# Each expert's rows spread by products on four row groups of the array, and five transfers and copies moved

## The reference

```python
def first_block(x, c, ...):
    mod = silu(c) @ w_ada + b_ada            # six rows: shift, scale, gate, twice
    h = rmsnorm(x, g_pre_mix) * (1 + scale_m) + shift_m
    # w_in projection; retention and dilated attention; mixed = [y_ret, y_att] @ w_out
    x = x + gate_m * rmsnorm(mixed, g_post_mix)
    h = rmsnorm(x, g_pre_ffn) * (1 + scale_f) + shift_f
    affinity = softmax(h @ w_router)                       # 16 experts
    gates, idx = top_k(affinity.T, 32)                     # each expert takes 32 tokens
    ye = (silu(h[idx] @ w_gate) * (h[idx] @ w_up)) @ w_down * gates
    moe = zeros_like(h).at[idx].add(ye)
    return x + gate_f * rmsnorm(moe, g_post_ffn)
# then, twice: half an FFN (1024 -> 2816 -> 1024), an mLSTM and windowed attention
# with a relative position bias, half an FFN, and a per-layer embedding.
```

## Time and profile before

| | before |
|---|---|
| three runs | 2316.99 to 2321.66 us, median 2320.9 |
| the profiled execution | 2319.57 us, its span 2317.8 us |
| PE, DVE, ACT busy | 81%, 46%, 30% of the span |
| mean granted clock of PE | 0.90 |
| HBM read | 656.6 MB, 284 GB/s over the span |

### The profile page before, as it was taken

One profiled execution on the slowest core, in us unless ns is written; L12 is line 12 of the kernel. 1 busy time (PEld: TensorE's weight loads), 2 busy tenths in 40 slices (PEclk: granted clock), 3 DMA queues, 4 the chain that ended last, 5 costly groups with the idle time before them and its releaser, 6 DMA issues.

```text
span 2317.8 us, 30979 instructions
## 1 busy us (share of the span) xinstructions
PE 1886.3 (81%) x11483; PEld 1285.3 (55%) x11483; DVE 1073.8 (46%) x1500; ACT 698.0 (30%) x965; POOL 43.3 (2%) x68
## 2 busy tenths in 40 slices
PE   6896765566555556556699999999999999999999
PEld 4774311111121112111388888788878888778887
DVE  3464100000000000000388877688868887777886
ACT  4331100000000000000344456454454445544444
POOL 0000000000000000000000010000000001000000
PEclk8996977777788877777899999999999999999999
DMA  9786999999999999999755654545545575444552
GB/s 368 259 321 275 429 429 428 429 428 429 428 428 428 428 429 428 429 428 429 310 191 181 234 178 128 175 153 179 201 146 191 172 241 179 136 142 165 184 189 83
DMA packets 174820, 660.83 MB, mean 285 GB/s; under 512 B 10051, under 2 KB 108140, under 8 KB 143732
## 3 DMA queue, kind: packets, MB, share of 16 engines
q1 hardware_dynamic: 171980, 654.12, 72.9%
q10 hardware_dynamic: 2376, 3.03, 0.6%
q0 software_dynamic: 352, 2.11, 0.3%
HBM read 656.60 MB, written 2.64 MB: 284 GB/s over the span
## 4 chain that ended last, share of the span: by engine, by line
PE 55%; DMA 38%; DVE 4%; ACT 2%; issue 1%; ACTq 0%; DVEq 0%; PEldq 0%; SPq 0%; PEld 0%
PE PS L1992 26%; DMA turned_and_rows<-in_w_down_e 13%; PE PS L2080 12%; DMA turned_and_rows<-in_w_gate_e 12%; DMA turned_and_rows<-in_w_up_e 11%; PE PS L2082 6%; PE PS L1948 3%; DVE arena L210 2%; PE PS L1671 2%; DVE units L210 1%; PE PS L1968 1%; DMA ring<-in_w_in 1%; DMA ring<-in_w_ada 1%; ACT units L210 1%; PE PS L2128 1%
## 5 line engine op out<-in xcount | busy, mean ns | idle before, releaser
L210 ACT ACTIVATE units<-ring 128x1024 fp32r<-128x1024 f32 (+2 forms) x416 | 438.4, 1054 | 489.9 <-PE PS L2082 266.4
L210 DVE TENSOR_TENSOR units<-ring,units 128x1024 fp32r<-128x1024 f32 (+2 forms) x416 | 505.9, 1216 | 117.1 <-ACT units L210 82.4
L2080 PE MATMUL PS<-hT_split,units 128*128 128x512 f32 x1216 | 432.4, 398 | 0.0
L210 DVE SCALAR_TENSOR_TENSOR arena<-arena,PS 128x512 f32<-128x512 f32 (+1 forms) x54 | 41.4, 768 | 770.6 <-ACT arena L210 489.6
L210 ACT ACTIVATE arena<-PS 128x512 f32<-128x512 f32 (+3 forms) x137 | 67.7, 494 | 919.9 <-PE PS L1956 309.4
L2082 PE MATMUL PS<-hT_split,units 128*128 128x256 f32 x1216 | 341.3, 281 | 0.0
L1992 PE MATMUL PS<-units,hT_split 128*128 128x512 f32 (+2 forms) x1248 | 285.1, 386 | 4.5 <-DVE hT_split L210 2.5
L2080 PEld LDWEIGHTS PS<-hT_split,units 128*128 128x128 f32 x1216 | 228.5, 188 | 55.9
L1992 PEld LDWEIGHTS PS<-units,hT_split 128*128 128x128 f32 x1248 | 230.5, 189 | 49.2 <-issue 4.4
L1992 PE MATMUL PS<-units,hid_split 128*128 128x512 f32 x1056 | 255.4, 391 | 0.0
L2082 PEld LDWEIGHTS PS<-hT_split,units 128*128 128x128 f32 x1216 | 229.6, 189 | 3.0
(11 more groups left out here) (214 smaller groups left out, 1430.8 us busy)
## 6 DMA issues: line engine op xcount, KB each, us to landing
ring<-in_ffn_wi SPq DMA_DIRECT2D x88, 1024.0 KB, 5.5
ring<-in_w_gate_e SPq DMA_DIRECT2D x24, 2048.0 KB, 36.7
moe_ring<-in_w_up_e SPq DMA_DIRECT2D x24, 2048.0 KB, 36.2
ring<-in_w_down_e SPq DMA_DIRECT2D x24, 2048.0 KB, 35.5
moe_ring<-in_w_gate_e SPq DMA_DIRECT2D x24, 2048.0 KB, 35.9
ring<-in_w_up_e SPq DMA_DIRECT2D x24, 2048.0 KB, 35.8
moe_ring<-in_w_down_e SPq DMA_DIRECT2D x24, 2048.0 KB, 36.2
ring<-in_ffn_wo SPq DMA_DIRECT2D x44, 1024.0 KB, 5.0
```

The source lines that it names most:

```text
L210: return instruction(*args, **kwargs)
L2080: first = mm(PS[:, bank, :].rearrange("p (i n) -> p i n", i=2), w[0], hT_split[:, :, k, :], start=(k == 0), stop=False, skip_group_check=True)
```

## The change

- **Combine.** Each expert's rows are added by themselves. ACT makes one 128x256 copy `Y_e` of bank 5, in which each quarter of the columns stays on its 32 partitions. DVE writes the expert's gated one-hot columns four times side by side (`gated_e`), PE transposes them into bank 5 beside the result, DVE copies them to `GT_e`. `combine(e)` is eight products of 32 rows, 128 columns and 256 moving columns, each on one of the four row groups, in two turns of four that write four banks, with a wait on PE itself between the turns. It stands between the next expert's up product and its down product; the last one follows the loop.
- **Gather.** The first group's token rows are fetched unturned by eight products of 512 columns, copied by ACT and DVE, and turned by eight transposes.
- **Bias copies.** The write to `skew` moves from ACT in the first stage to SP in the first layer's `layer_constants`; DVE keeps a copy of `rep` for it in `p_rows`. The loads of `band`, `w_ple` and `pT` move behind the last FFN step's fills, into `layer_tables`, where SP waits for `skew_written`.
- **Stream.** SP waits for `ret_y`, issues `w_router`, and waits for both broadcast modulation rows before the first expert fill. ACT no longer issues `w_router`.
- **Order.** ACT's `first_hi(16, 17)` moves behind `att_copy(2)`, DVE's `first_lo(16, 17)` behind `att_scores(3)`.

```diff
+        rep_kept = p_rows.rearrange("p t n -> p (t n)")[0:SW_H, 0:3 * P]
...
-        GT = router.take(NQ, TOK)
+        e_hT = router.take(4, P)
+        gated_e = router.take(NT, 4 * CAP)
+        GT_e = router.take(TOK)
...
-        e_hT = gated[:, 0, :, :].rearrange("p e c -> p (e c)").rearrange("p (s n) -> p s n", s=4)
+        group_rows = gated.rearrange("p t e c -> p (t e c)")
...
-        Y = moe.take(D)
-        GT_group = moe.take(TOK)
+        Y_e = moe.take(TOK)
...
 
+            sp.wait_ge(S["ret_y"], 1)
+            sp.dma_start(w_router, a["w_router"][0].rearrange("(p k) e -> p k e", k=KT)).then_inc(S["router_full"], 16)
+            sp.wait_ge(S["mod_full"], 32)
...
                 def layer_constants():
-                    sp.wait_ge(S["skew_written"], 16)
-                    sp.dma_start(band, bass.AP(skew.tensor, P, [[3 * P - 1, P], [3 * P * P, SW_H], [1, TOK]])).then_inc(
-                        S["band_full"], 16)
+                    if l == 0:
+                        sp.wait_ge(S["rep_copied"], 2)
+                        sp.dma_start(skew.rearrange("h p n -> h p n"), rep_kept.unsqueeze(1).to_broadcast(
+                            [SW_H, P, 3 * P])).then_inc(S["skew_written"], 16)
...
+                def layer_tables():
+                    sp.wait_ge(S["skew_written"], 16)
+                    sp.dma_start(band, bass.AP(skew.tensor, P, [[3 * P - 1, P], [3 * P * P, SW_H], [1, TOK]])).then_inc(
+                        S["band_full"], 16)
                     sp.dma_start(w_ple, a["w_ple_2"][l].rearrange("(j p) n -> p j n", p=P)).then_inc(S["ple_full"], 16)
                     sp.dma_start(pT, a["p_2"][l, 0].rearrange("(j p) n -> p j n", p=P)).then_inc(S["ple_full"], 16)
 
...
                 ffn(POS_LAYER + OFF_FFN1, "ffn1_wi_2", "ffn1_wo_2", layer_constants)
+                layer_tables()
...
-            act.wait_ge(S["rep_copied"], 1)
-            program.dma_start(skew.rearrange("h p n -> h p n"), rep.unsqueeze(1).to_broadcast([SW_H, P, 3 * P])).then_inc(
-                S["skew_written"], 16)
...
             att_exp(1)
             att_copy(0)
...
-                    first_hi(18, 19)
+                    first_hi(16, 17, 18, 19)
                 elif h == 6:
...
-                if t == 0:
-                    program.dma_start(w_router, a["w_router"][0].rearrange("(p k) e -> p k e", k=KT)).then_inc(
-                        S["router_full"], 16)
...
+            act.wait_ge(S["gathered"], 1)
+            activation(group_rows[:, 0:512], PS[:, 6, :], ACT.Copy).then_inc(S["xeT"], 1)
...
-            act.wait_ge(S["gathered"], 2 + KT + 1)
-            activation(GT.rearrange("p q n -> p (q n)"), two_banks(0), ACT.Copy).then_inc(S["GT"], 1)
+            act.wait_ge(S["gathered"], 4 + KT)
 
...
                     act.wait_ge(S["big_used"], before + EXPERT_SLOTS)
-                    if r == 0:
-                        act.wait_ge(S["combined"], q + 1)
-                    for g in range(4):
-                        last = activation(Y[32 * r:32 * r + 32, 256 * g:256 * g + 256],
-                                          PS[32 * g:32 * g + 32, 5, 0:256], ACT.Copy)
-                    last.then_inc(S["y_copied"], 1)
+                    activation(Y_e, PS[:, 5, 0:TOK], ACT.Copy).then_inc(S["y_copied"], 1)
 
             hidden_rows(0)
             for q in act.loop(NQ, 1):
...
-            first_lo(16, 17)
             att_scores(3)
-            first_lo(18, 19)
+            first_lo(16, 17, 18, 19)
             att_scores(4)
...
+            dve.wait_ge(S["rep_copied"], 1)
+            dve.run(V.tensor_copy, rep_kept, rep).then_inc(S["rep_copied"], 1)
...
+            dve.wait_ge(S["gathered"], 2)
+            dve.run(V.tensor_copy, group_rows[:, 512:D], PS[:, 7, :]).then_inc(S["xeT"], 1)
...
 
-                dve.wait_ge(S["combined"], q + 1)
-                dve.run(V.tensor_copy, GT_group, GT[:, bass.ds(q, 1), :].rearrange("p q n -> p (q n)")).then_inc(
-                    S["GT_group"], 1)
...
                         dve.run(V.tensor_copy, xe, xeT[:, :, bass.ds(e * CAP, CAP)]).then_inc(S["xe"], 1)
+                    dve.run(V.tensor_copy, gated_e.rearrange("p t (g c) -> p t g c", g=4),
+                            gated[:, :, bass.ds(e, 1), :].to_broadcast([P, NT, 4, CAP])).then_inc(S["GT"], 1)
...
                     stt(e_act, e_tanh, 1.0, PS[:, 2, :], ALU.add, ALU.mult)
                     dve.wait_ge(S["big_used"], BIG + q * GROUP_SLOTS + r * EXPERT_SLOTS + KT)
                     stt(e_hid, e_act, 0.5, PS[:, 3, :], ALU.mult, ALU.mult).then_inc(S["e_hid"], 1)
-
-            dve.wait_ge(S["GT"], 1)
...
             hidden_rows(0)
             for q in dve.loop(NQ, 1):
...
@@ -1899,32 +1903,46 @@
                 return last
 
             for half in range(2):
-                for k in range(4):
-                    last = gather(PS[:, 6 + half, k * P:(k + 1) * P], 4 * half + k, 0, GROUP)
+                for t in range(NT):
+                    for i in range(2):
+                        last = mm(PS[:, 6 + half, :], onehot_rounded[:, t, 0:GROUP, :].rearrange("p e c -> p (e c)"),
+                                  hn_split[:, i, t, 512 * half:512 * half + 512], start=(t + i == 0), stop=(t + i == NT))
                 last.then_inc(S["gathered"], 1)
+            pe.wait_ge(S["xeT"], 2)
+            for k in range(KT):
+                last = nc.tensor.transpose(PS[:, 6 + k // 4, (k % 4) * P:(k % 4 + 1) * P], group_rows[:, k:D:KT], ident)
+                if k % 4 == 3:
+                    last.then_inc(S["gathered"], 1)
 
             def gather_rest():
 
                 pe.wait_ge(S["selected"], 4)
-                pe.wait_ge(S["xeT"], 1)
+                pe.wait_ge(S["xeT"], 3)
                 for k in range(KT):
                     if k == 4:
-                        pe.wait_ge(S["xeT"], 1 + 4)
+                        pe.wait_ge(S["xeT"], 3 + 4)
                     gather(PS[:, LATE_BANK[k % 4], 0:NE * CAP - P], k, GROUP, NE).then_inc(S["gathered"], 1)
-                pe.wait_ge(S["xeT"], 1 + KT)
-                pe.wait_ge(S["selected"], 5)
-                for q in range(NQ):
-                    for t in range(NT):
-                        last = nc.tensor.transpose(
-                            PS[:, q // 2, (q % 2) * TOK + t * P:(q % 2) * TOK + (t + 1) * P],
-                            gated[:, t, GROUP * q:GROUP * q + GROUP, :].rearrange("p e c -> p (e c)"), ident)
-                last.then_inc(S["gathered"], 1)
-
-            def open_sums():
-
-                pe.wait_ge(S["GT"], 1)
+                pe.wait_ge(S["xeT"], 3 + KT)
                 for bank in LATE_BANK:
                     mm(PS[:, bank, 0:2], zeros[0:1, 0:P], zeros[0:1, 0:2], start=True, stop=False, skip_group_check=True)
+
+            def combine(e, signals=(None, None)):
+
+                pe.wait_ge(S["GT_group"], e + 1)
+                pe.wait_ge(S["y_copied"], e + 1)
+                for turn in range(2):
+                    if turn == 1:
+                        last.then_inc(S["gathered"], 1)
+                        pe.wait_ge(S["gathered"], 4 + KT + 2 * e + 2)
+                    for t in range(NT):
+                        for n in range(2):
+                            g = 2 * n + (t + turn) % 2
+                            rows = slice(32 * g, 32 * g + 32)
+                            last = mm(PS[:, 6 * t + n, TOK * (g % 2):TOK * (g % 2) + TOK], GT_e[rows, t * P:(t + 1) * P],
+                                      Y_e[rows, :], start=False, stop=False, skip_group_check=True,
+                                      tile_position=(32 * g, 0))
+                        if turn == 1 and signals[t] is not None:
+                            last.then_inc(S[signals[t]], 1)
 
             def experts(q):
 
...
+                    else:
+                        combine(e - 1)
+                    pe.wait_ge(S["GT"], e + 1)
+                    for t in range(NT):
+                        last = nc.tensor.transpose(PS[:, 5, TOK + t * P:TOK + (t + 1) * P], gated_e[:, t, :], ident)
+                    last.then_inc(S["gathered"], 1)
                     pe.wait_ge(S["e_hid"], e + 1)
...
-                    if r > 0:
-                        pe.wait_ge(S["y_copied"], e)
+                    pe.wait_ge(S["GT_group"], e + 1)
                     for j in range(4):
                         at = r * EXPERT_SLOTS + KT + j
...
-                    if alone and r == 0:
-                        open_sums()
-                pe.wait_ge(S["GT_group"], q + 1)
-                pe.wait_ge(S["y_copied"], (q + 1) * GROUP)
-                for t in range(NT):
-                    for n in range(2):
-                        last = mm(PS[:, 6 * t + n, :], GT_group[:, t * P:(t + 1) * P], Y[:, 512 * n:512 * n + 512],
-                                  start=False, stop=False, skip_group_check=True)
-                    last.then_inc(S["combined" if t == 1 else "combined_first"], 1)
 
```

(9 more changed lines are left out.)

8 lines of the change are left out of this document (3 added, 5 removed).

## The result

The changed kernel takes 2325.75 us (median of 14 runs, 2323.0 to 2329.3) against 2321.03 for the kernel before on the same chips (14 runs, 2317.0 to 2323.6): ratio 1.0021, 95% interval 1.0014 to 1.0028. So it is 4.7 us slower, where 2.1 us faster was forecast. The profiled execution took 2324.21 (before: 2319.57); its span is 2322.4 and its mean granted clock 0.906 (before 0.899).

What follows compares the result with a forecast made beforehand. DMA was taken to bound the expert stream, PE the later layers, the chain of waits the first stage. Terms -13.8 - 1.3 + 13.0 = -2.1 us, from the median 2320.9 to 2318.8; 8-in-10 range 2304 to 2331.

Steps and rivals of the forecast that it cites:

- Part 1: First stage: without the skew write and with the new order, rv's products start and end earlier; net gain 6.1 us.
- if the clock falls all the same the gain is 5: First stage, rv's products: gain of 5 us in place of 6.5 if the clock drops despite the shorter gap.
- two idle microseconds should not do that: First stage, before rv's products: a gap of two us should not lower the clock, so they take 5.72 us.
- Part 2: Routing ahead of the experts: modulation rows meet an idle DMA and router weights come early; gain 6.5 us.
- Part 3: Gather ahead of the first expert: 6.9 to 7.0 us against 8.3; gain 1.2 us, with 0 and 3 as ends.
- The stream: Experts' weight stream: starts 13.8 us earlier (6.1 + 6.5 + 1.2), its length left as it was.
- Part 4: Last combine, at the stream's end: gain 1.3 us, losses up to 2 possible if reconfiguring the array stops it.
- Part 5: First layer's FFN: fills queue behind the skew write; PE stands 10.5 us plus 2.5 for the clock, cost 13.0 us.
- the first fill lands at about 1322.7: First layer's FFN, last step: the write runs to about 1320, the first fill lands then, PE restarts at about 1325.1.
- The estimate that the prediction drew from a page: Skew write in the FFN: eight partitions reach two ports, so 54 GB/s, 29 us of write, 11 us stall with clock.
- The first, that the write does not hold PE up: First layer's FFN: engines skip ahead or the write is quick alone; -15.1 us, 2305.8 us; chance 0.10.
- The slower rival: First layer's FFN: write takes longer than 38 us, stall costs over 20, time 2326 to 2336 us; chance 0.16.

Runs made afterwards that it cites:

- e1: The changed kernel with the skew write issued by ACT in the first stage again, as before: 2306.84 us, ratio 0.9942.
- e2: The kernel before with only the bias copies changed (skew write by SP in the first layer's FFN): 2331.94 us, ratio 1.0048.
- e9: The kernel before with only the order of first_hi and first_lo of 16 to 19 changed: 2316.74 us, ratio 0.9979.
- e10: The kernel before with only the stream's part: router weights on SP's queue, wait for modulation rows ahead of expert fills: 2310.79 us, ratio 0.9951.
- e3: The changed kernel with the write's same 1536 KB read from 128 partitions in place of eight, other values: 2305.43 us, ratio 0.9937.
- e5: The changed kernel with the same values and bytes written from 64 partitions in place of eight: 2305.26 us, ratio 0.9939.
- e8: The changed kernel with the eight-partition write issued by ACT at the start of the first layer's first FFN, not by SP: 2314.99 us, ratio 0.9975.
- e12: e5 with the combine alone as before the change: 2308.20 us, ratio 0.9938.
- e11: The changed kernel with the write behind the ten small tables, still ahead of the FFN's last three fills: 2325.62 us, ratio 1.0014.
- e13: The changed kernel with half of the write, 768 KB from the same eight partitions, band read with other values: 2310.67 us, ratio 0.9954.
- e6: e5 with gather and combine as before the change: 2308.36 us, ratio 0.9957.
- e7: e5 with the gather alone as before the change: 2309.84 us, ratio 0.9959.

## Why the prediction was wrong

**Part 1, right in its size, with one doubt confirmed.** Reckoned 6.1, 5.2 by rv's start, and 4.5 at the end of the attention part. The clock did not stay up: the 7.32 us were the case named beside the estimate ("if the clock falls all the same the gain is 5"). What e1, e2 and e9 add is that the reorder and the removal of the write are two cures for one wait: either brings PE back by 99.3, and together they don't add. The prediction gave the gain to both. The better cure was the removal alone: in e2 PE is back at 94.66 with the clock at full, and 9.6 us reach the end of the attention part, where the changed kernel has 4.5. The 2.3 us that the prediction charged for the reorder became a gap of 2.5 us and a fallen clock, the one that its sentence "two idle microseconds should not do that" had ruled out.

**Part 2, right in its place, too small in its size.** 6.5 reckoned. In the changed kernel the gather starts 12.6 us earlier, of which 4.5 were there at the end of the attention part: 8.1 for this part, as in e10. The two parts together were reckoned at 12.6 and measured at 12.6, which is luck: the first was 1.6 short and the second 1.6 over.

**Part 3, right where the clock was as supposed.** Reckoned 6.9 to 7.0 us from the gather's start to the first expert product; 6.9 in e1, e3, e5, e8 and e12, where the transposes run at half clock (1.97 us), and 5.8 in the changed kernel, e11 and e13, where they find it up (1.16). So the gain there is 1.4 or 2.5, against 1.2. The term left out that the first expert product would also find the clock coming up: 5.36 to 6.62 us in the eight traces with the new gather, 6.69 to 8.15 in the six with the old one.

**The stream** started 13.8 us earlier by the sum, and 15.1 at the first expert product and 15.8 at the last down product by the trace.

**Part 4, right for the chain** (1.3 reckoned, 1.7 by the trace), but 3.8 us were lost beside it to half clock in the last down product and the first FFN product. With the old combine this happens in some traces: the FFN product takes 6.0 to 6.1 us before, in e6 and in e10, and 7.7 to 8.5 in e2, e9 and e12. With the new one it takes 8.0 to 8.5 in all eight traces. e6 and e7 differ in the combine alone; e6 has

```profile
1136.74 6.08 PE L1999 MATMUL PS<-hT_split,units 128*128 128x256 f32 x48 [0.56 <-DVE hT_split L210]
```

and e7 8.02 us. The prediction left the stream's end at what it cost before, and that failed by those 3.8. Whether the new combine has a part in them is open.

**Part 5, the step that failed.** It had the right place, chain of waits (ACT for the fill, DVE, PE) and length of the write: 0.21 MB in each 4 us, drained at about 1307, 33 us after its issue against 32 reckoned. The term that was mis-sized is the one behind it, "the first fill lands at about 1322.7", 2.7 us after the write's end. The fill landed 8 us after it, because SP had not been able to issue it before: from the write's issue to ACT's use of the fill it was 41.2 us, against 34.8 reckoned. That SP's issues would be held is a wait that the prediction did not have. Idle time 16.6 in place of 10.5, clock 1.6 in place of 2.5, and 1.6 of smaller waits that had no term, together **19.8 in place of 13.0**. e11, where a fill was being issued right behind the write, had 36.4, and took the 5 us by which the tables had gone first off again. That is the whole of it: -15.1 + 13.0 became -13.7 + 19.8, and 6.8 of the 6.8 us between forecast and result are this term; the front's smaller misses and the 1.5 us of clock in the profiled execution before cancel.

The estimate that the prediction drew from a page (29 us of write, 11 of stall with clock) was no better for the stall. The rule itself, the Trainium skill, SBUF — State Buffer, Door 1, agrees with the traces in this: from 64 and from 128 partitions, which by it reach eight and sixteen ports, the same bytes landed 10.2 and 9.6 us after issue, in place of some 33 from eight partitions. The two landings are nearly the same, and each write ran beside the fill issued just before it, so what sixteen ports give over eight these runs do not show.

**The rivals.** The first, that the write does not hold PE up, was priced at 2305.8, and e3 and e5 measured 2305.4 and 2305.3: that is what the change is worth without its slow write. The slower rival had the right side and the wrong mechanism: it asked for a write of over 38 us, and a write of 33 was enough.

**What stays open:** the worth of the combine, in time and in clock; 2.5 us of e10's gain and what the medians give the gather beyond 2.2 us; whether e5 with the former order is faster still; and what exactly in the engines holds a fill up beside the write (e8 shows that it happens across queues, not where).

## What to carry to other kernels

A DMA out of few partitions is paid by its time and not by its bytes: it holds up the issuing queue and the fills on other queues too. Either give it more source partitions (here eight copies of the rows, made by a product that ran anyway) or put it where nothing is due for as long as it runs; moving it to another place in the queue gave back nothing, to another queue and place half. When two edits both remove one wait, try each alone before adding them up: here the costly one was not needed, and e1, the change without it, is 0.6% faster than the kernel before. And when a sum comes out to the tenth, check its terms: the first two were 1.6 us off, each the other way.

## What the runs showed of the hardware

- SP's issue of a load of 4 KB or less took 3 to 10.3 us while a 1536 KB write from eight partitions was draining in its queue (0.3 to 0.6 before), a pair of 1 MB fills 25.9 (1.3 in e5), and a single fill 11.8 with the write in ACT's queue (0.38 without it).
- Beside that write (50 GB/s at a 42 to 45% share of the engines) two 1 MB fills on another queue moved 0.31 MB in the 4 us behind their issue, with 28% of the engines' time, and landed after 29.1 us. From 1160 to 1168 the next fill moved 0.13 MB in 4 us, with 9%.
- The clock fell to half behind an idle stretch of 2.5 us at 98 us (products 7.32 us for 5.72), and did not in e2, where the products followed at once (5.74).
- Eight products of 32 rows by 256 columns on four row groups, written to four banks, took 1.51 us in two turns (16 entries at full clock), against 3.70 for the four products of 128 rows by 512 before (eight entries).
